# Norms and handovers in a two-block network: epsilon as the root's bias, tiles normalised in halves, constants loaded late, ring places returned at turns

## The reference

```python
for i in range(DEPTH):                       # DEPTH = 2
    x = _layer_norm(a * x + MACARON_W * _swiglu(x, ffn_w1[i, 0], ffn_w3[i, 0], ffn_w2[i, 0]), ln_g[i, 0], ln_b[i, 0])
    mix = token_mixing(...)      # RWKV-7, gated linear attention, gated delta rule
    x = _layer_norm(a * x + mix, ln_g[i, 1], ln_b[i, 1])
    x = _layer_norm(a * x + MACARON_W * _swiglu(x, ffn_w1[i, 1], ffn_w3[i, 1], ffn_w2[i, 1]), ln_g[i, 2], ln_b[i, 2])
    ple = jax.nn.sigmoid(x @ ple_w_gate[i]) * (p[i] @ ple_w_proj[i])
    x = _layer_norm(a * x + ple, ln_g[i, 3], ln_b[i, 3])
```

## Time and profile before

| | |
|---|---|
| median of 3 runs | 3180.95 us (3176.93 to 3181.07) |
| the profiled execution, its own time | 3184.92 us |
| its span, first to last instruction | 3183.1 us |
| mean granted TensorE clock | 0.984 of full |
| busy: PE, PE weight load, DVE, ACT, POOL | 95%, 74%, 55%, 21%, 1% |
| DMA | 430 MB, 135 GB/s over the span |

### The profile page before, as it was taken

One profiled execution on the slowest core, in us unless ns is written; L12 is line 12 of the kernel. 1 busy time (PEld: TensorE's weight loads), 2 busy tenths in 40 slices (PEclk: granted clock), 3 DMA queues, 4 the chain that ended last, 5 costly groups with the idle time before them and its releaser, 6 DMA issues. The chain is left out here.

```text
span 3183.1 us, 52421 instructions
## 1 busy us (share of the span) xinstructions
PE 3013.5 (95%) x22638; PEld 2345.8 (74%) x22638; DVE 1760.8 (55%) x2612; ACT 683.4 (21%) x1310; POOL 40.7 (1%) x80
## 2 busy tenths in 40 slices
PE   8999988999999999999899999989999999988998
PEld 8987764559976998674467995555888885555897
DVE  5554555556555564555456566584334663196665
ACT  1102113112112101212212103271111002144210
POOL 1000000000001000000000000000000000000000
PEclk9999999999999999999999999999999999999999
DMA  8645312227646746323216744201222442231442
GB/s 277 220 170 183 132 48 101 80 80 231 212 159 211 245 171 208 132 68 107 80 54 218 246 150 149 80 1 53 80 96 89 146 166 92 80 106 60 159 159 106
DMA packets 279638, 430.34 MB, mean 135 GB/s; under 512 B 9944, under 2 KB 147520, under 8 KB 279408
## 3 DMA queue, kind: packets, MB, share of 16 engines
q1 hardware_dynamic: 273920, 411.52, 38.1%
q0 software_dynamic: 5024, 14.34, 1.4%
q10 hardware_dynamic: 464, 1.12, 0.1%
HBM read 425.91 MB, written 1.05 MB: 134 GB/s over the span
## 5 line engine op out<-in xcount | busy, mean ns | idle before, releaser
L455 PE MATMUL bank<-xT,ring 128*128 128x128 f32 (+3 forms) x4608 | 787.0, 330 | 10.5 <-DVE arena L825 5.7
L455 PE MATMUL bank<-arena 64*64 64x64 f32 (+9 forms) x7244 | 732.9, 283 | 47.6 <-DVEq L4032 8.5
L455 PEld LDWEIGHTS bank<-xT,ring 128*128 128x128 f32 (+1 forms) x4608 | 676.7, 192 | 113.7 <-issue 54.8
L455 PEld LDWEIGHTS bank<-arena 128*128 128x128 f32 (+4 forms) x7244 | 632.9, 163 | 146.6 <-issue 31.5
L455 PE MATMUL bank<-ring,xT 128*128 128x512 f32 (+2 forms) x1536 | 578.9, 549 | 7.7 <-DMA ring<-in_ple_w_gate 3.5
L455 PE MATMUL bank<-ring,arena 128*128 128x256 f32 (+1 forms) x1584 | 447.3, 435 | 17.7 <-DVE arena L882 6.5
L455 PEld LDWEIGHTS bank<-ring,xT 128*128 128x128 f32 (+1 forms) x1536 | 257.0, 183 | 271.5 <-issue 252.4
L455 PEld LDWEIGHTS bank<-ring,arena 128*128 128x128 f32 x1584 | 302.0, 193 | 135.2 <-issue 87.3
L825 DVE TENSOR_TENSOR arena<-arena,bank 128x256 f32<-128x256 f32 (+1 forms) x198 | 92.2, 466 | 399.3 <-PE bank L455 259.8
L736 ACT COPY arena<-bank 128x256 f32<-128x256 f32 (+1 forms) x264 | 107.8, 408 | 749.5 <-PE bank L455 748.0
L785 DVE TENSOR_TENSOR arena<-ring,arena 128x1024 f32<-128x1024 f32 (+1 forms) x216 | 257.1, 1190 | 7.4
(11 more groups left out here) (391 smaller groups left out, 2104.6 us busy)
## 6 DMA issues: line engine op xcount, KB each, us to landing
ring<-in_ffn_w SPq DMA_DIRECT2D x88, 1024.0 KB, 8.0
ring<-in_w_in SPq DMA_DIRECT2D x32, 2048.0 KB, 7.8
ring<-in_ffn_w_in SPq DMA_DIRECT2D x44, 1024.0 KB, 6.8
arena<-in_ada_w SPq DMA_DIRECT2D x20, 2048.0 KB, 13.4
ring<-in_ffn_w SPq DMA_DIRECT2D x16, 2048.0 KB, 8.0
ring<-in_ffn_w_out SPq DMA_DIRECT2D x12, 2048.0 KB, 8.0
ring<-in_hgrn_w_in SPq DMA_DIRECT2D x12, 2048.0 KB, 7.8
ring<-in_ffn_w SPq DMA_DIRECT2D x8, 1536.0 KB, 6.8
```

Source lines behind the costliest of these rows:

```text
L455: return self.e.matmul(o, lhsT, rhs, start=start, stop=stop, skip_group_check=True)
```

## The change

1. Epsilon is no longer added on VectorE. Two columns of `small` are set once, and ScalarE's Sqrt takes them as its bias.
2. The normalisation of a tile is issued as two halves of 512 columns. Each raises `x_ready` or `xn_ready`, and TensorE waits before each group of four turns (`pe_norm_mod` still waits for all of them).
3. In half 1 of an FFN the sum with `acc[4]` is issued between tile 0's statistics and the wait for its root (`meanwhile`).
4. The identity is a transfer of its own, first on ACT's queue, and x comes as one transfer per tile. POOL waits for the second tile before it issues the rest of the constants in two transfers, and for block 1 of the ring before its `lnp` rows. `consts_landed` is waited for behind the first FFN, and for the conditions' zeroes not at all: they are made from the identity.
5. `pe_turn_c` and `act_turn_c` move from ahead of the first FFN to its block 1, the wait for `c_cols_ready` to block 2. ScalarE copies one column early, so its table is loaded then.
6. `release` is also called at the first turn of a tile or group.
7. In the last FFN the sums for tile 1 are joined before `apply` (`join_last`).
8. At the end POOL multiplies the left halves by the weight once they are complete, ScalarE scales them, VectorE does the right halves, and each tile is stored by a transfer of its own.

The core of the diff; semaphore declarations, waits that only follow a changed count, and call sites that only pass an argument on are left out.

```diff
-            eng.wait_ge(result_ready, 2)
-            eng.dma_start(out[0].rearrange("(t p) d -> p t d", p=P), xtok[:]).then_inc(result_stored, 16)
-            eng.wait_ge(result_stored, 16)
+            for tt in range(2):
+                eng.wait_ge(left_half_done, tt + 1)
+                eng.wait_ge(right_half_done, tt + 1)
+                eng.dma_start(out[0, tt * P:(tt + 1) * P, :], xtok[:, tt]).then_inc(result_stored, 16)
+            eng.wait_ge(result_stored, 32)
...
-                pe.wait_ge(x_ready, pe.due(x_ready))
                 for q in range(2):
+                    pe.wait_ge(x_ready, pe.due(x_ready))
...
                         mm = pe.turn(bank[:, k * P:(k + 1) * P], src[:, kt * P:(kt + 1) * P])
+                        if k == 0:
+                            pe.release(mm)
...
-                apply(s, half % 2, 1, acc[7].unsqueeze(1).broadcast_to([P, 2, 256]), True)
+                def sum_4():
+                    dve.wait_ge(down_products, 7 * h + 6)
+                    add(w.sum[:, 1, 0:256], w.u, acc[4])
+
+                rows0 = w.sum[:, 0].rearrange("p (a n) -> p a n", a=2)
+                if half % 2:
+                    apply(s, 1, 0, rows0, True, sum_4)
+                else:
+                    apply(s, 0, 0, rows0, True)
+                    sum_4()
+                rows1, last_product = w.sum[:, 1].rearrange("p (a n) -> p a n", a=2), acc[7].unsqueeze(1).broadcast_to([P, 2, 256])
+                if join_last and half == last:
+                    dve.wait_ge(down_products, 7 * h + 7)
+                    add(rows1, last_product, rows1)
+                    apply(s, half % 2, 1, rows1, True)
+                else:
+                    apply(s, half % 2, 1, rows1, False)
+                    dve.wait_ge(down_products, 7 * h + 7)
+                    apply(s, half % 2, 1, last_product, True)
...
-        def dve_normalize(dve, x, tt):
+        def dve_normalize(dve, x, tt, meanwhile=None):
...
-            v.bn_aggr(small[:, 0:2], stats[:, tt]).then_inc(dve_step, dve.up(dve_step))
-            dve.wait_ge(dve_step, dve.sent(dve_step))
-            ins = v.tensor_scalar(small[:, 2:3], small[:, 1:2], LN_EPS, None, ALU.add)
-            ins.then_inc(var_ready, dve.up(var_ready))
+            v.bn_aggr(small[:, 0:2], stats[:, tt]).then_inc(var_ready, dve.up(var_ready))
             dve.wait_ge(var_ready, dve.sent(var_ready))
+            if meanwhile:
+                meanwhile()
             dve.wait_ge(std_ready, dve.due(std_ready))
             v.reciprocal(small[:, 4:5], small[:, 3:4]).then_inc(dve_step, dve.up(dve_step))
             dve.wait_ge(dve_step, dve.sent(dve_step))
-            ins = v.tensor_scalar(x, x, small[:, 0:1], small[:, 4:5], ALU.subtract, ALU.mult)
-            ins.then_inc(dve_step, dve.up(dve_step))
-            dve.wait_ge(dve_step, dve.sent(dve_step))
+            for q in range(2):
+                half = x[:, 512 * q:512 * q + 512]
+                ins = v.tensor_scalar(half, half, small[:, 0:1], small[:, 4:5], ALU.subtract, ALU.mult)
+                ins.then_inc(x_ready, dve.up(x_ready))
+            dve.wait_ge(x_ready, dve.sent(x_ready))
...
-        def act_std(act, n=2):
+        def act_std(act, n=2, rms=False):
+            var, eps = (small[:, 2:3], EPS_RMS) if rms else (small[:, 1:2], EPS_LN)
             for _ in range(n):
                 act.wait_ge(var_ready, act.due(var_ready))
-                act.e.activation(small[:, 3:4], small[:, 2:3], ACT.Sqrt).then_inc(std_ready, act.up(std_ready))
+                act.e.activation(small[:, 3:4], var, ACT.Sqrt, bias=eps).then_inc(std_ready, act.up(std_ready))
                 act.wait_ge(std_ready, act.sent(std_ready))
...
+            ins = act.e.activation(cst[:, LVL0 + P:LVL0 + 3 * P].rearrange("p (a m) -> p a m", a=2),
+                                   ident.unsqueeze(1).broadcast_to([P, 2, P]), ACT.Identity, scale=0.0)
+            ins.then_inc(act_step, act.up(act_step))
+            act.wait_ge(act_step, act.sent(act_step))
...
-            act.e.dma_start(xtok[:], a["x"][0].rearrange("(t p) d -> p t d", p=P)).then_inc(x_landed, 16)
+            act.e.dma_start(cst[:, 0:P], a["cst"][:, 0:P]).then_inc(ident_landed, 16)
+            for tt, landed in enumerate((x_landed, second_x_landed)):
+                act.e.dma_start(xtok[:, tt], a["x"][0, tt * P:(tt + 1) * P, :]).then_inc(landed, 16)
...
+                pe.wait_ge(xn_ready, pe.due(xn_ready))
                 ring_ = to_dve if last and q else to_act
                 pe.wait_ge(ring_.freed, ring_.next_free())
...
+                    if j == 0:
+                        pe.release(mm)
...
+        def dve_rstd(dve, tt, out_=small[:, 4:5], done=dve_step, meanwhile=None):
...
-            ins = v.tensor_scalar(small[:, 1:2], small[:, 1:2], HEAD_EPS, None, ALU.add)
...
-        def dve_norm_tile(dve, s, tt, homes=None):
-            dve_rstd(dve, 2 * s + tt)
-            ins = nc.vector.tensor_scalar((homes or xn)[s][:, tt], stream_tok[s][:, tt], small[:, 4:5], None, ALU.mult)
-            ins.then_inc(dve_step, dve.up(dve_step))
-            dve.wait_ge(dve_step, dve.sent(dve_step))
-            dve.sem_inc(xn_ready, dve.up(xn_ready))
+            v.reciprocal(out_, small[:, 3:4]).then_inc(done, dve.up(done))
+            dve.wait_ge(done, dve.sent(done))
+
+        def dve_norm_tile(dve, s, tt, homes=None, meanwhile=None):
+            dve_rstd(dve, 2 * s + tt, meanwhile=meanwhile)
+            for q in range(2):
+                c_ = slice(512 * q, 512 * q + 512)
+                ins = nc.vector.tensor_scalar((homes or xn)[s][:, tt, c_], stream_tok[s][:, tt, c_], small[:, 4:5], None,
+                                              ALU.mult)
+                ins.then_inc(xn_ready, dve.up(xn_ready))
+            dve.wait_ge(xn_ready, dve.sent(xn_ready))
...
                     if half and norm:
-                        dve_norm_tile(dve, s, tt, norm)
+                        dve_norm_tile(dve, s, tt, norm, meanwhile)
+                    elif meanwhile:
+                        meanwhile()
+                    if final and half == 0:
+                        dve.sem_inc(left_half_ready, dve.up(left_half_ready))
...
             dve.wait_ge(final_norm_landed, dve.due(final_norm_landed, 16))
+            dve_ffn7(dve, ffn_gated_residual(dve, gtmp7, final=True),
+                     lambda b: None if b else dve_gate_diagonals(dve, 1, GT2, (0,), diag7), join_last=True)
             for tt in range(2):
-                dve_rstd(dve, tt)
-                ins = v.scalar_tensor_tensor(out=xtok[:, tt], in0=xtok[:, tt], scalar=small[:, 4:5], in1=lnp[:, 1],
-                                                    op0=ALU.mult, op1=ALU.mult)
-                ins.then_inc(result_ready, dve.up(result_ready))
-                dve.wait_ge(result_ready, dve.sent(result_ready))
+                dve_final_scale(dve, tt)
+
+        FINAL_SCALE = [small[:, 5:6], small[:, 6:7]]
+
+        def dve_final_scale(dve, tt):
+
+            dve_rstd(dve, tt, FINAL_SCALE[tt], scale_ready)
+            x = xtok[:, tt, 512:D]
+            ins = nc.vector.scalar_tensor_tensor(out=x, in0=x, scalar=FINAL_SCALE[tt], in1=lnp[:, 1, 512:D],
+                                                 op0=ALU.mult, op1=ALU.mult)
+            ins.then_inc(right_half_done, dve.up(right_half_done))
+            dve.wait_ge(right_half_done, dve.sent(right_half_done))
+
+        def pool_final_weights(pool):
+
+            pool.wait_ge(final_norm_landed, pool.due(final_norm_landed, 16))
+            for tt in range(2):
+                pool.wait_ge(left_half_ready, pool.due(left_half_ready))
+                x = xtok[:, tt, 0:512]
+                ins = pool.e.tensor_tensor(x, x, lnp[:, 1, 0:512], ALU.mult)
+                ins.then_inc(left_half_weighed, pool.up(left_half_weighed))
+                pool.wait_ge(left_half_weighed, pool.sent(left_half_weighed))
+
+        def act_final_scale(act, tt):
+
+            act.wait_ge(left_half_weighed, act.due(left_half_weighed))
+            act.wait_ge(scale_ready, act.due(scale_ready))
+            x = xtok[:, tt, 0:512]
+            ins = act.e.activation(x, x, ACT.Copy, scale=FINAL_SCALE[tt])
+            ins.then_inc(left_half_done, act.up(left_half_done))
+            act.wait_ge(left_half_done, act.sent(left_half_done))
...
-            act_turn_c(act)
             for l in range(DEPTH):
                 ada = [ffn_ada(marks, lambda: act_ada_product(act, True), lambda: act_ada_turn(act)) for marks in IN_FFN[l]]
+                if l == 0:
+                    ada[0] = with_conditions(ada[0], lambda: act_turn_c(act), lambda: None)
                 act_ffn7(act, ada[0])
+                if l == 0:
+                    act.wait_ge(consts_landed, act.due(consts_landed, 32))
...
-            e.dma_start(cst[:], a["cst"]).then_inc(consts_landed, 16)
+            pool.wait_ge(second_x_landed, 16)
```

(7 more changed lines are left out.)

100 lines of the change are left out of this document (53 added, 47 removed).

## The result

The changed kernel takes 3163.88 us, the median of four executions (3163.18 to 3164.54), against 3181.01 for the kernel before: a ratio of 0.9949 with an interval of 0.9932 to 0.9966. In a second comparison the same kernel took 3158.71 (five executions, 3158.23 to 3163.25) and the kernel before 3179.78: 0.9941 (0.9928 to 0.9953). So it is faster, by 17 us in one comparison and by 21 in the other. The nine executions of the changed kernel and the 42 of the kernel before that were timed beside it and its variants (3175.2 to 3183.5) do not overlap.

A forecast was written before the change was run, and what follows sets the result against it. TensorE, busy 3013.5 of 3183.1 us, was taken as the bound, so only its gaps pay. Terms 4.3 + 3.5 + 1.9 + 1.0 + 3.5 = 14.2 us gave a median of 3166.8, range 3160.5 to 3173.

The forecast's parts named there:

- start, to the first FFN's statistics: Start: first product at 12.8 instead of 17.61 us, less condition turns at block 1; 4.3 us, bounds 0 and 4.8.
- ring's place: PLE of layer 0: place returned at first turn, `in_ple_w_gate` issued 12 us earlier, 3.52 us wait goes; bounds 2.5 and 3.5.
- four FFN ends: At 235, 939, 1212, 1918 us: TensorE resumes about 0.5 us earlier at each; 1.9 us in all, bounds 0 and 3.
- two handovers: PLE to FFN (997 us) and HGRN to FFN (2963 us): constant gone, first half turned early; 0.5 each, 1.0 us.
- end: Program's end: joined sums, no constant, halves, last store issued 2.2 us earlier with 1.35 left; 3.5 us, bounds 2.2 and 3.6.
- Block 0 by the sharing of packets: Start: queues share by packets, so with POOL's loads held back the ring's block 0 lands at 12.7 us.
- the clock's part: First 32 products: about 3 us of idling again, so the loss of 2.9 us stays; bounds 3 better, 3 worse.
- Block 0 no earlier: Rival at the start: something other than the sharing of packets bounds block 0; 3171.0 us, chance 0.15.
- the ring's wait moved: Rival: the ring's wait only moves to the next block or another holder of SyncE; 3170.3 us, chance 0.07.
- most of it off the path: Rival: TensorE falls due elsewhere, leaving only the end's 3.5 us and a little; 3176 us, chance 0.06.
- The clock's help: Rival: higher clock returns 3 us sooner at the start or a fall elsewhere is missed; 3161 to 3164, chance 0.12.

The follow-up runs named there:

- a1: The changed kernel again, unaltered, on another chip: 3158.71 us (3158.23 to 3163.25).
- b1: The changed kernel without POOL's two waits, so its constants and lnp rows are issued at once as before: 3168.02 us (3164.82 to 3170.32).
- b3: The changed kernel without the three releases at turns, ring places given back at first products only: 3169.83 us (3165.60 to 3170.79).
- c4: The changed kernel with a tile normalised by one instruction over 1024 columns instead of two halves: 3162.02 us (3161.65 to 3164.32).

## Why the prediction was right, step by step

It was right: 3163.88 against 3166.8, in the range, faster as forecast. That it lay in the range was in part luck, since the same kernel's second median, 3158.71, does not; the terms bear it out better. Each by the stretch that shows it (before, then changed):

| term | predicted | measured | from |
|---|---|---|---|
| start, to the first FFN's statistics | 4.3 | 5.65 | 235.83 to 230.18 |
| ring's place | 3.5 | 3.2 | projection to gate 12.83, 9.64 |
| four FFN ends | 1.9 | 2.6 | last product to next block: 12.36, 12.35, 12.08, 8.77 become 11.59 (a1), 11.62, 11.51, 8.21 (a1) |
| two handovers | 1.0 | 0.55 | 16.63, 16.01 become 16.42, 15.67 |
| end | 3.5 | 3.3 | sum with `acc[4]` to the end: 13.70, 10.38 |
| sum | 14.2 | 15.3 | |

The rest of the 20.9 us, 5.6, lies at falls of the clock: with the two traces laid over each other by TensorE's instructions, the lead of the changed kernel changes (but for 0.1 us near 1975) only at the places of the table and where one of the two has a fall. Most came in the token mixing: the lead grew by 2.8 us between 254 and 666 us, where two falls of 6.8 us became 3.4 (at 563 and 611 before), and by about 5.3 between 1220 and 1687, where six falls of 27.3 us together became five of 17.1. A new fall at 238, and one more and one longer in the second network, took some back. Part of the 5.6 is the choice of executions. The profiled one of the kernel before, at 3184.92, is slower than any other that was timed; the mean spans, 3177.9 us over 38 executions before and 3160.1 over nine of the changed kernel, are 17.8 apart.

- **Start.** Block 0 by the sharing of packets: forecast at 12.7, waited for until 12.70; b1 confirms it by undoing that alone. The 0.45 us of turns at block 1 was right too. What was mis-sized is the clock's part: I kept all of the earlier trace rows's slow first 32 products (6.66), and they took 5.50 and in a1 3.81. I had expected some 3 us of idling ahead of them again, as before, where a recorded fall came at 16.7, behind 2.3 us of it, and lasted to 23.6. TensorE idled 1.08 and 1.24 us, and no fall came: the half level of the start ended at 16.2, with 16 of the 32 done, and in a1 at 11.1, ahead of them all. The earlier trace rows was read rightly; the 1.00 that the rows print for the changed kernel's start is no contradiction, since no record stands there.
- **Ring.** The issue came at 933.81, 8.9 us ahead of the projection's product, where it stood 2.1 behind it before (953.10 and 950.99): 11.0 us earlier in the program's course, 12 forecast. The gap of 3.52 went, and b3 brings 3.06 back.
- **FFN ends.** The size was low, and its working had errors of opposite sign. The root takes 0.09 more, since I had put the bias at nothing. The two halves take 1.00 together (1.04 forecast), and of the 0.15 that I allowed between them and tile 1's update 0.04 is left; so that update came 0.47 earlier behind tile 0's aggregate (0.32 forecast), and tile 1's root 0.66 (0.51 forecast). The four ends gained 0.66 each on average. But the halves have next to no part in it: c4 is 0.1 better without them at three of the four. The gain is the addition removed and the sum put into the root's wait; no run takes these two apart. I had worked out 0.52 from the earlier trace rows and set that against the figure of the Trainium skill (VectorE: DVE Perf Modes, the section on the TRN2 errata, a fixed 0.156 us where my row had 0.22). By 1.00 - 0.81 the second instruction costs 0.19 us when it follows the first at once, between the two (one half alone lasts 0.54, which makes it an estimated 0.28, of which 0.09 overlaps), and the skill's warning against splitting held at three of these four places.
- **Handovers.** This term failed in size, 0.55 for 1.0. Halves gave 0.34 and 0.33 as c4 shows, more than the 0.3 in my sum. What did not come is the rest, 0.2 at each for the addition removed: c4, which has everything but the halves, stands level with the kernel before at the HGRN (16.01 both) and 0.13 behind it at the PLE (16.76 against 16.63). The root's 0.09 takes half of it back, which leaves 0.08 in TensorE's gap (1.36 to 1.28, 0.81 to 0.73), and the next stop, for VectorE's sums (L808), takes that: its wait grew from 0.87 to 0.95 at the HGRN and from 0.95 to 1.15 at the PLE. It is 1.15 in c4 too, so the halves' earlier turns are not the cause. At the PLE ScalarE's first eviction starts 1.02 us behind the first turn, and 0.74 before the change; why is open. I had not asked what TensorE waits for next.
- **End.** Every term was within 0.1: 0.75 for the half, 1.4 for the second store, 0.72 for ScalarE. The dearer root takes 0.09 twice.
- **The rivals.** Block 0 no earlier, the ring's wait moved, and most of it off the path are refuted by their own rows. The clock's help, to which I had given 0.12 and 3161 to 3164, did happen beside the forecast: 3163.88 is in that range as well as in the forecast's own. It was wrong to hold the two apart. Its part at the start, 1.2 us and in a1 2.9, goes with the shorter idling there; the rest is a scatter of some 5 us that every median here carries.

What stays open: why the mixing's falls are shorter in the changed kernel. The two executions of one and the same kernel show that four falls of twenty come and go at places that the program doesn't change; whether the change made them rarer, or each profile met a lucky pattern, fourteen traces don't settle. Over all executions the mean granted clock was 0.986 before (38) and 0.987 changed (nine), about 4.5 us of what could be lost, and the fall at the start, which the one trace before has and no trace of the changed kernel, makes 3.4 of that. That gaps of about 1 us at an FFN's end bring one on is shown for one place only.
